# Filler matmuls and gate work of a two-block forward pass moved into the first half of the sparse-attention loop

## What is computed

```python
ya = sigmoid(p["m_o"]) * mh * silu(p["m_z"])          # mh: mLSTM output, normalised per head
...
s_s = einsum(q_rope, k_selected) * scale               # selected blocks: all 8 blocks of 64 keys at most
p_s = softmax(where(kpos <= tq, s_s, NEG))
s_w = einsum(q_rope, k_window) * scale                 # window of 512 keys
p_w = softmax(where(causal, s_w, NEG))
out = g0 * o_c + g1 * (p_s @ v_s) + g2 * (p_w @ v_w)
yb  = out * silu(p["n_z"])
merged = sigmoid(p["g_a"]) * (ya @ w_branch_a) + sigmoid(p["g_b"]) * (yb @ w_branch_b)
```

## Time and profile before

| what | us |
|---|---|
| time before, median of 3 runs | 2085.69 (2083.81 to 2085.92) |
| time of the profiled execution | 2085.69 |
| its span in the trace | 2084.0 |
| matmul busy time in the span | 1990.6 (96%) |
| VectorE busy | 994.8 (48%) |
| ScalarE busy | 794.1 (38%) |
| stretch of the 64 units, from the first score to the first merge tile | 388.63 to 555.26 |

### The profile page before, as it was taken

One profiled execution on the slowest core, in us unless ns is written; L12 is line 12 of the kernel. 1 busy time (PEld: TensorE's weight loads), 2 busy tenths in 40 slices (PEclk: granted clock), 3 DMA queues, 4 the chain that ended last, 5 costly groups with the idle time before them and its releaser, 6 DMA issues.

```text
span 2084.0 us, 25850 instructions
## 1 busy us (share of the span) xinstructions
PE 1990.6 (96%) x9406; PEld 1627.3 (78%) x9406; DVE 994.8 (48%) x1409; ACT 794.1 (38%) x1335; POOL 171.0 (8%) x192
## 2 busy tenths in 40 slices
PE   6999999999999999999999889999899999999998
PEld 5888778766778877888887777799688878888886
DVE  5688666553343444333333758734543443333332
ACT  3334333444332334444322555334422334434332
POOL 1101110000000020000001120023200010000010
PEclk9999999999999999999999999999999999999999
DMA  8967812100033423333333313320233423333331
GB/s 294 301 178 241 275 36 90 41 26 21 26 81 96 146 61 92 100 91 101 98 96 85 104 43 94 84 56 11 76 96 101 138 69 104 94 96 100 91 101 51
DMA packets 329617, 212.80 MB, mean 102 GB/s; under 512 B 21245, under 2 KB 315066, under 8 KB 328894
## 3 DMA queue, kind: packets, MB, share of 16 engines
q1 hardware_dynamic: 318016, 170.58, 28.3%
q0 software_dynamic: 10368, 37.75, 5.1%
q10 hardware_dynamic: 1150, 3.35, 0.4%
HBM read 204.31 MB, written 7.35 MB: 102 GB/s over the span
## 4 chain that ended last, share of the span: by engine, by line
PE 81%; DVE 10%; ACT 3%; issue 2%; DMA 2%; ACTq 1%; POOL 0%; DVEq 0%; SPq 0%; POOLq 0%
PE psum L429 23%; PE psum L430 23%; PE psum L431 23%; DVE delta_qkv_T L1978 2%; DMA ada_w<-in_ada_w 2%; PE psum L1100 2%; PE psum L1308 1%; DVE w_lo L388 1%; DVE ada_sum L1978 1%; PE psum L1124 1%; PE psum L1111 1%; PE psum L987 1%; PE psum L1003 1%; ACT w_hi L380 1%; PE psum L1254 1%
## 5 line engine op out<-in xcount | busy, mean ns | idle before, releaser
L429 PE MATMUL psum<-act_hi,w_hi 128*128 128x512 f32 x1616 | 649.8, 402 | 15.4 <-DVE act_lo L1978 5.7
L431 PE MATMUL psum<-act_hi,w_lo 128*128 128x512 f32 x1616 | 634.4, 393 | 0.0
L430 PE MATMUL psum<-act_lo,w_hi 128*128 128x512 f32 x1616 | 634.4, 393 | 0.0
L388 DVE TENSOR_TENSOR w_lo<-w_raw,w_hi 128x1024 fp32r<-128x1024 f32 x306 | 386.0, 1266 | 381.3 <-ACT w_hi L380 359.2
L380 ACT ACTIVATE w_hi<-w_raw 128x1024 fp32r<-128x1024 f32 x306 | 320.0, 1053 | 194.6 <-PE psum L431 181.4
L429 PEld LDWEIGHTS psum<-act_hi,w_hi 128*128 128x128 f32 x1616 | 306.7, 190 | 94.3 <-issue 26.0
L431 PEld LDWEIGHTS psum<-act_hi,w_lo 128*128 128x128 f32 x1616 | 306.3, 190 | 65.9
L430 PEld LDWEIGHTS psum<-act_lo,w_hi 128*128 128x128 f32 x1616 | 306.7, 190 | 62.1 <-issue 1.2
L705 POOL TENSOR_TENSOR squares<-squares 128x512 f32<-128x512 f32 x30 | 46.3, 1551 | 1314.8 <-ACT squares L1495 911.0
L429 PE MATMUL psum<-ffn_hi,w_hi 128*128 128x512 f32 x352 | 139.6, 396 | 0.0
L431 PE MATMUL psum<-ffn_hi,w_lo 128*128 128x512 f32 x352 | 139.0, 395 | 0.0
(11 more groups left out here) (341 smaller groups left out, 2423.7 us busy)
## 6 DMA issues: line engine op xcount, KB each, us to landing
w_raw<-in_ffn_w_in SPq DMA_DIRECT2D x88, 512.0 KB, 3.8
ada_w<-in_ada_w POOLq DMA_DIRECT2D x72, 512.0 KB, 5.5
w_raw<-in_w_in SPq DMA_DIRECT2D x68, 512.0 KB, 3.9
w_raw<-in_mix_w_in SPq DMA_DIRECT2D x52, 512.0 KB, 3.7
w_raw<-in_ffn_w_out SPq DMA_DIRECT2D x32, 512.0 KB, 4.0
w_raw<-in_ffn_w_out SPq DMA_DIRECT2D x16, 384.0 KB, 3.4
w_raw<-in_w_branch_a SPq DMA_DIRECT2D x8, 512.0 KB, 3.9
residual<-x_away SPq DMA_DIRECT2D x2, 2048.0 KB, 8.5
```

Source lines behind the costliest of these rows:

```text
L388: dve.tensor_tensor(WLO[:, n % 4, :], RAW[:, n % 4, :], WHI[:, n % 4, :].bitcast(F32), ALU.subtract).then_inc(w_lo, 1)
L429: pe.matmul(out, whi, hhi, start=start, stop=False)
L430: pe.matmul(out, whi, hlo, start=False, stop=False)
L431: return pe.matmul(out, wlo, hhi, start=False, stop=stop)
```

## The change

Three schedules of the loop are rewritten; no instruction's operands change.

- PE issues a quarter in each of the units 0 to 31 and none in 32 to 63. Before, it issued one in every even unit of the 64.
- ACT and DVE do `gate_tile` 12 to 19 in units 4, 8, ..., 32. Before, it was 12 to 18 in units 8, 16, ..., 56 and 19 after the last unit.
- The eight `ya`, `ya_hi` and `ya_lo` move to units 2 to 20, two units apart mostly. Before, they were four apart, in units 2 to 36.

```diff
@@ PE
-                if u < len(units) and u % 2 == 0:
+                if u < 32:
                     oz(1)
@@ ACT
-            YA_AT = {3: 0, 7: 1, 11: 2, 15: 3, 19: 4, 23: 5, 27: 6, 35: 7}
+            YA_AT = {3: 0, 5: 1, 7: 2, 9: 3, 11: 4, 13: 5, 15: 6, 19: 7}
...
-                if u % 8 == 0 and u:
-                    gate_tile(11 + u // 8)
+                if u % 4 == 0 and 4 <= u <= 32:
+                    gate_tile(11 + u // 4)
                 if u in YA_AT:
                     ya_hi(YA_AT[u])
             turned(len(units) - 2)
-            gate_tile(19)
             turned(len(units) - 1)
@@ DVE
-            YA_AT = {2: 0, 6: 1, 10: 2, 14: 3, 18: 4, 22: 5, 26: 6, 34: 7}
-            YA_LO_AT = {4: 0, 8: 1, 12: 2, 16: 3, 20: 4, 24: 5, 28: 6, 36: 7}
+            YA_AT = {2: 0, 4: 1, 6: 2, 8: 3, 10: 4, 12: 5, 14: 6, 18: 7}
+            YA_LO_AT = {4: 0, 6: 1, 8: 2, 10: 3, 12: 4, 14: 5, 16: 6, 20: 7}
...
-                if u % 8 == 0 and u:
-                    gate_tile(11 + u // 8)
+                if u % 4 == 0 and 4 <= u <= 32:
+                    gate_tile(11 + u // 4)
                 if u in YA_LO_AT:
                     ya_lo(YA_LO_AT[u])
                 if u in YA_AT:
                     ya(YA_AT[u])
                 if u >= 7 and (u - 7) % 4 == 0:
                     add_branch((u - 7) // 4)
-            gate_tile(19)
             add_branch(15)
```

## The result

The changed kernel takes 2141.29 us (median of 4 runs, 2140.23 to 2143.20) against 2085.81 for the kernel before beside it (4 runs, 2083.81 to 2086.77): ratio 1.0268, with a 95% interval of 1.025 to 1.0286. The forecast was 2082.3 with a range to 2086.8. It missed by 59 us, on the other side. The loss comes with every execution of the changed kernel: the profiled one and the four others have spans of 2138.6 to 2142.3 us and mean granted clocks of 0.949 to 0.952, where the executions of the kernel before have about 0.98.

A forecast was written before the change was run, and what follows sets the result against it. TensorE, with matmuls busy 96% of the span, was taken as the bound. Stalls -1.6, units without quarters +0.1 and clock -1.9 summed to -3.4, so 2085.7 became 2082.3 us, range 2079.0 to 2086.8.

The forecast's parts named there:

- The cost of a moved quarter: In the attention loop, each quarter moved to another unit takes its plain matmul time of 1.43 us along.
- The stalls of the gate tiles: PE waits where gate tiles are inserted, opening included: 6.2 us together against 7.8 before, 1.6 won, bounds 0 and 3.
- units 20 to 28: Gate tiles 16, 17 and 18: waits of 0 to 1.0 us each, 0.6 taken for the three.
- The opening: Start of the loop: quarters at units 1 and 3 cover the first two waits, cost 0.
- the bare units: Units 33 to 63, without a quarter: stalls only by tenths, 0 to 1.5 us in all, 0.1 taken.
- splits: Weight splits every four units in the loop, raw chunks requested four tiles earlier: hidden, cost 0.
- The shorter of the two expected falls: Low clock after the 1.9 us wait at unit 8: six chances in ten, price 1.5 us.
- no fall at all: Rival: all waits in the loop stay below 2 us and the clock never falls, 2079.6 us; chance 0.14.
- The clock: Waits at units 8 and 32 may each lower PE's clock, six in ten: 2.7 us against 4.6, 1.9 won.
- The third rival: From unit 33 on, work without quarters is too light for full clock: 2105 us with half the units slow; chance 0.08.
- The second rival: Units 0 to 31 get too dense with DVE inserts, eight gate tiles cost 9.6 us: 2087.5 us; chance 0.13.

The follow-up runs named there:

- the first experiment: The changed kernel with gate tile 19 moved from unit 32 back behind the last unit: 2080.53 us (10 runs), ratio 0.9964 to the kernel before.
- experiment 2: The changed kernel with the last tile's four quarters in units 48 to 51 instead of 28 to 31, gate tile 18 at unit 32, 19 last: 2106.49 us.
- the fourth experiment: The kernel before with quarters at units 1, 2, 3 and 5 of each eight and three `ya_lo` moved off gate units: 2080.53 us, ratio 0.9967.
- the burst at unit 48: The same kernel as experiment 2, four quarters in units 48 to 51 of the changed kernel: 2106.49 us, one run.

## Why the prediction was wrong

**What held.** The cost of a moved quarter: 16 of them at 1.43 are 22.9 us, and units 0 to 31 grew by 22.45. The stalls of the gate tiles: I had 0.5, 1.9, 0.5, 1.15 and 1.5 us for units 4, 8, 12, 16 and 32; the trace has idle times of 0.34, 1.75, 0.35, 0.98 and 1.43, and with the 0.16 that each costs on top these are 0.50, 1.91, 0.51, 1.14 and 1.59. For units 20 to 28 I had 0.6 and there is nothing. The opening costs nothing, the bare units don't stall, and neither splits nor DMA are late. In all there are 5.0 us of waits in 6 places where there were 7.3 in 8. The shorter of the two expected falls, behind unit 8, came too and at its price: from that wait to the next one are 11.2 us in the changed kernel and 9.7 in the first experiment, where the clock held, so 1.5 as forecast. The rest of the sum stands as well: the first experiment, with neither fall, is 6.8 us below the kernel before beside it (2080.53 against 2087.29), where "no fall at all" had 6.1.

**What failed is the step "The clock".** It gave the fall at unit 32 six chances in ten and a price of 3.1 us. The fall came; it cost 57.7 us in the loop (against the first experiment) and about 2.4 behind it. That the loop grew by only 53.4 is because the rest of the change had won something. The price was copied from 462.6 to 469.4, after the stall of the same unit in the kernel before. But that stretch ended with a quarter that began at 465.69, and in the changed kernel no quarter stands behind unit 31. I carried over the length of a low stretch without asking what ended it. The experiments with one group of six matmuls show that the ending is part of the price: with the first group at unit 36 the low stretch is 10 us (479.6 to 489.7), with the first at unit 40 it is 24 (479.8 to 503.7), with the first late quarter at unit 48 it is 51, and with none 133 us (480.0 to 613.1), which ends in the first 512-column matmuls behind the loop. Priced so, the step would have read: fourteen bare units of 384 keys at 3.35 - 1.94 = 1.41 us and sixteen of 512 at the 1.75 that the third rival has, 19.7 + 28.0 = 48 us. All of it stood in the rows and the diff, and at six chances in ten it is a forecast of slower, not of no change. (The rows of after have 1.64 and about 2.2 a unit. The three steps of the earlier trace rows began at 462.34, before the fall, so part of them still ran at the full clock, and the 512-key price was estimated without a row.)

**The third rival** named the right rows and nearly the right price (2105 for half of the units, which makes some 2130 for all), but its reason was wrong and I gave it 0.08. It asked whether the bare stream is too light to hold the clock, and the evidence against it, half the units bare at 1.00, was sound: with gate tile 19 at unit 44 the clock held through 12 bare units, with its wait covered through 29, and with it at the end through 32. It didn't ask the other question, whether the stream can recover the clock. The evidence for it that I set aside, that the fall with bare units around lasted twice as long as the other, was the trace's own hint at that.

The Trainium skill ("TensorE: Matmul & The Clock Gate", part 4, PE-mode transpose) says that the full clock does not engage for transposes. The traces here disagree. In the first experiment the bare units, of whose time transposes take some 18% (0.35 of 1.93 us), stood at 1.00 for 40 us on end. And there is a stretch of transposes alone, which the prediction overlooked: the 32 of line 770 near the start of the program, with nothing else on PE. Of the changed kernel, its first six and its last eleven (count: duration in ns, shortest/median/longest; first and last start):

```profile
L770 PE MATMUL psum<-constants,x_normed x6: 421/421/473, 16.3 to 17.5; 128*128 128x128 f32 x6
...
L770 PE MATMUL psum<-constants,x_normed x11: 272/272/328, 20.0 to 21.4; 128*128 128x128 f32 x11
```

The transposes of line 1111 last 0.42 us at the low level and 0.27 at the full one, so the clock rose during this stretch. (The trace's clock entries begin only there; ahead of them a window prints 1.00.) The same change of length shows in all 13 traces, 2.8 to 6.0 us after the first of the 32. So transposes by themselves raise the clock. Why the mixed stream of scores, transposes and 64-column products doesn't regain it is open: no run takes the scores and the products apart.

The Trainium skill ("TensorE: Matmul & The Clock Gate", part 1, What's actually happening) puts the ramp's penalty at under 1% of a typical kernel's span. That is another case than the one here, a fall in the middle of the program that lasts: 133 us at the low level, 6.2% of the span, in a kernel that took 2.7% longer.

**The second rival**, a first half that gets too dense, was not borne out: that half lost nothing.

## What to carry to other kernels

Before filler is taken out of a stretch, ask of each wait left in it not only how long it is but what stands behind it to bring the clock back; a price for a low stretch read from a trace holds only as far as the matmuls that ended it are still there. Filler is worth most just behind the inserts that stall PE: here two groups of six matmuls at the right place were worth 56 us. And when PE's busy time grows while its counts stay the same, look at the clock line before anything else.

## What the runs showed of the hardware

- TensorE's clock in a stream of 64-row scores, 128-column transposes and 64-column products depends on its past. It stayed at 1.00 (2.4 GHz) for 32 units when it came in at 1.00, and at 0.50 (1.2 GHz) for some 30 units, 133 us with almost no idle time, when a wait of 1.43 us had brought it down.
- Waits of 1.43, 1.42 and 1.20 us among bare units brought it down each time (six kernels); 0.80 among units of 512 keys (one execution) and 0.18 did not. Among quarters the size didn't decide: nine of the profiled executions have the same wait of 1.74 to 1.78 at unit 8, and the clock fell behind it in five (a mean of 0.79 from 412 to 420 us in the changed kernel) and held in four (the first experiment is one). What decided there is open. A short low stretch (0.59 over 4 us) stood in the fourth experiment 2 us behind a wait of only 0.35, which I can't explain.
- From the first 512-column matmul behind a low stretch to the full clock it took 3.7 us in the kernel before (465.7 to 469.4), 3.8 and 4.1 with one group of six 128x512 matmuls, 4.6 in the burst at unit 48, and 5.0 in the merge stage of the changed kernel.
- A stretch of 32 transposes with nothing else on TensorE went from the low to the full level in all 13 traces (durations from 0.42 to 0.27 us), 2.8 to 6.0 us after its first.
- More work made the changed kernel faster four times: by 40 us with 96 extra matmuls, by 45 with 24, by 46 with 42, and by 56 with 12.
